# Squares of the residual and their sums, one to three positions later in the feed-forward pair of the second token half

## The chip, the cores and the metric

The kernel runs on one core of one Trainium2 chip. The metric is the device time of one execution in microseconds (us).

## The reference

One step of a decoder layer over 544 tokens: 512 of a new sequence and 8 x 4 tokens of running ones. What matters here is its second half (token mixing before it ends in `mix`, a matrix product):

```python
x = x + rmsnorm(mix, g_mix_post)
h = rmsnorm(x, g_ffn_pre)            # x * rsqrt(mean(x*x) + eps) * g
gt = h @ w_gate                      # 2048 -> 5632
c = conv_b + sum(ext(gt)[j] * conv_w[j] for j in range(3))
f = gelu(c) * (h @ w_up)
x = x + rmsnorm(f @ w_down, g_ffn_post)
```

## The kernel before

Activations lie with the 2048 model channels on the partitions, as 16 tiles (`kt`) of 128 x 544 tokens. Every fp32 product is made as three fast ones: weights and activations are split into a rounded part (`w_hi`, `act_hi`) and a rest (`w_lo`, `act_lo`), and `act_hi*w_hi`, `act_lo*w_hi` and `act_hi*w_lo` are summed in PSUM. Weights come in *units* of 128 x 512 numbers (two `kt` of a 256-column group), through a ring of four buffers: SP loads a unit, ACT makes `w_hi` (`split_hi`, line 358), DVE makes `w_lo` (`split_lo`, line 364), PE runs 24 matmuls of 272 columns on it. The buffers turn round: SP loads unit k+4 when DVE has split unit k, and ACT splits unit k+3 only when PE has used unit k-1 (`unit_used`).

Each engine has its own instruction queue, whose order is written out by hand: loops over positions k = 0 to 15, each of which begins with the split of unit k+3 (`LEAD` = 3) and then carries other work. Engines meet only at semaphores.

The change lies in the first feed-forward pair, 16 units that belong to two column groups (gate and up of 128 columns each). `PAIR` lays them out: units 0, 2, 4, 6, 8 and 10, 11, 12 are of the even group (banks `ps_acc`), 1, 3, 5, 7, 9 and 13, 14, 15 of the odd one (banks `ps_a`, `ps_b`). An even unit brings two new activation tiles (unit 8 needs kt 8 and 9, units 10, 11 and 12 need 10 to 15), an odd unit uses tiles that are there already. Units 0 to 3 run on the first token half, then on the second.

Beside this pair, the activations of the *second token half* (272 tokens) are prepared, in eight steps j = 0 to 7 of two tiles each:

- DVE `x2_pair(1, j)` (lines 1575, 1578): residual x2 = normalized mix + x.
- ACT `x2_hi(1, j)` (line 739): `act_hi` = rounded x2 * gain.
- DVE `x2_lo(1, j)` (line 1584): `act_lo`; this releases PE (`act_ready`).
- ACT `x2_squares(1, j)` (line 751): the squares of x2, into one of two buffers, `sq[:, j % 2]`.
- DVE `x2_add(1, j)` (line 1593 for j = 0, a copy; line 1596 for the others): adds them to `x2_sum`.

The buffers tie the last two: squares of j wait until the add of j-2 has read the buffer.

```python
def x2_squares(i, j):
    ...
        act.wait_ge(x2_added, 8 + max(j - 1, 0))
        dst = sq[:, j % 2]
```

The norm of the feed-forward input isn't applied to the activations but to the products: when all squares are summed, PE adds them over the partitions (`x2_sums`, line 939, after unit 12), DVE and ACT make the reciprocal root (`mean_square`, `root`, `root_mean`), PE spreads it (`spread_rstd`, line 910, after unit 13), DVE copies it to `rstd` (`rstd_in`, line 1235), and `gate_tail` (lines 1638 to 1661) takes the first gate and up products out of `ps_acc`, with the convolution, the GELU and the product. Then PE may use those banks again, from unit 16 on.

Of the kernel before, what the change touches and what calls it, by code (L numbers as in the profile page):

```python
# [74 lines left out]
PAIR_END = 12  # L75
# [72 lines left out]


FIRST_AT = {8 + 6 * j: j for j in range(8)}  # L150
ADD_AT = (1, 2, 4, 5, 7, 9, 11, 12)


ROWS_AT = {8 * s + 2 * mt + 1: s - 2 + mt for s in (2, 4, 6, 8) for mt in range(2)}
# [3 lines left out]
def build(nc, xT, units, kcache, vcache, table, gains, pool_hist, conv_par, rope_tab, consts,  # L158
          yT, kT_out, vT_out, ext_out, tail_out):
    with ExitStack() as ctx:  # L160
# [226 lines left out]
        def two(ap):  # L387
            return ap.rearrange("p (a n) -> p a n", a=2)
# [93 lines left out]
        def _(act):  # L482
# [259 lines left out]
            def x2_squares(i, j):  # L742

                if i == 0:
                    if j:
                        act.wait_ge(x2_added, j)
                    dst = sq_x
                else:
                    act.wait_ge(x2_added, 8 + max(j - 1, 0))
                    dst = sq[:, j % 2]  # L750
                act.activation(two(dst), x2[:, 2 * j:2 * j + 2, half_of(i)], ACT.Square).then_inc(x2_sq, 1)
# [32 lines left out]
            def chunk(c, first=False, last=False):  # L784
                q0 = c * Q_CH + Q_FF
                g0 = c * G_CH + G_FF

                def gate_group(j, before=None):
                    for u in range(8):
                        split_hi(act, 2 * j + q0, u + LEAD)  # L790
                        if before is not None and u == 1:
                            ff_gate(g0 + before, before)
                            f_part(before, before)
                    F = c * CH + j
                    ff_gate(j + g0, F)
                    f_part(F, j)
                if first:
                    split_hi(act, q0, LEAD)
                    half_out(HALVES - 1)
                    root(3, 4)  # L800
                    x2_hi(1, 0)
                    x2_hi(1, 1)
                    x2_squares(1, 0)
                    x2_squares(1, 1)
                    x2_hi(1, 2)
                    for k in range(1, 16):
                        split_hi(act, q0, k + LEAD)
                        if k == 1:
                            x2_squares(1, 2)
                        if k in (2, 4, 6, 8, 10):  # L810
                            x2_hi(1, k // 2 + 2)
                        if k in (3, 5, 7, 9, 11):
                            x2_squares(1, k // 2 + 2)
                        if k == PAIR_END:
                            root(4)
                        if k == PAIR_END + 2:
                            ff_gate(g0, 0)
                            f_part(0, 0)

                    gate_group(2, before=1)  # L820
                    gate_group(3)
                else:
                    with act.Fori(0, CH) as j:
                        gate_group(j)
                with act.Fori(0, 3 if last else 4) as d:
                    for k in range(4):
                        split_hi(act, d + q0 + 2 * CH, k + LEAD)
                    if last:
                        for i in range(4):
                            last_squares(4 * d + i, i % 2)  # L830
                if last:
                    split_hi(act, q0 + 2 * CH + 3, LEAD)
                    for i in range(4):
                        last_squares(12 + i, i % 2)
# [15 lines left out]
        def _(pe):  # L850
# [121 lines left out]
            def pair_halves(G, q):  # L972

                for k in (1, 0, 2, 3):
                    pair_half(q, k, 0)
                    if k == 0:
                        half_sums(1)
                half_spread(1)
                for k in range(4):
                    pair_half(q, k, 1).then_inc(unit_used, 1)  # L980
                for k in range(4, 16):
                    odd, u = PAIR[k]
                    ff_unit(G + odd, q, k, u, 8, act_hi, act_lo, odd, None if odd else lambda kt: (act_ready, 3 * KT + kt + 1))
                    if k == PAIR_END:
                        x2_sums()
                    if k == PAIR_END + 1:
                        spread_rstd(4)

            def pair_groups(G, q, n, ready):
# [217 lines left out]
        def _(dve):  # L1207
# [24 lines left out]
            def rstd_in(n):  # L1232

                dve.wait_ge(spread_done, n)
                dve.tensor_copy(rstd[:, :].rearrange("p (a n) -> p a n", a=4),
                                ps[:, :, :, HN:HN + NT // 4].rearrange("p a b n -> p (a b) n"))
                dve.drain().then_inc(rstd_ready, 1)
# [349 lines left out]
            def x2_add(i, j):  # L1587

                s = x2_sum[:, :, half_of(i)]
                dve.wait_ge(x2_sq, 8 * i + j + 1)  # L1590
                src = two(sq[:, j % 2] if i else sq_x)
                if j == 0:
                    dve.tensor_copy(s, src).then_inc(x2_added, 1)
                else:
                    dve.drain()
                    dve.tensor_tensor(s, s, src, ALU.add).then_inc(x2_added, 1)
# [67 lines left out]
            def chunk(c, first=False, last=False):  # L1664
                q0, g0 = c * Q_CH + Q_FF, c * G_CH + G_FF
                if first:
                    split_lo(dve, q0, LEAD)
                    add_half(HALVES - 1)
                    mean_square(3, ps[0:TOK, 0, 1, 0:4])
                    root_mean(3, 4)  # L1670
                    rstd_half(1)
                    x2_pair(1, 0)
                    x2_lo(1, 0)
                    x2_pair(1, 1)
                    x2_lo(1, 1)
                    x2_pair(1, 2)
                    for k in range(1, 16):
                        split_lo(dve, q0, k + LEAD)
                        if k in (1, 3, 5, 7, 9, 11):
                            x2_lo(1, k // 2 + 2)  # L1680
                        if k in (2, 4, 6, 8, 10):
                            x2_pair(1, k // 2 + 2)
                        if k in ADD_AT:
                            x2_add(1, ADD_AT.index(k))
                        if k == PAIR_END:
                            mean_square(4)
                        if k == PAIR_END + 1:
                            root_mean(4)
                            rstd_in(4)
                        if k == PAIR_END + 2:  # L1690
                            gate_tail(c, 0, 0, q0, PAIR_END)

                    gate_group(c, 2, 0, pair=True)
                    gate_group(c, 2, 1)
                else:
                    with dve.Fori(0, CH // 2) as j:
                        for odd in range(2):
                            gate_group(c, 2 * j, odd)

                def down(d, ahead):  # L1700
                    for k in range(4):
                        if k < ahead:
                            split_lo(dve, d + q0 + 2 * CH, k + LEAD)
                        if k >= 2:
                            for mt in range(2):
                                i, g = k - 2, 2 * d + g0 + CH + k - 2
                                t = tile_of(acc, 4 * d + 2 * i + mt)
                                tile_done(dve, g, mt, d + q0 + 2 * CH, k)
                                if first:
                                    o = dve.tensor_copy(two(t), bank(mt, i))  # L1710
                                else:
                                    o = dve.tensor_tensor(two(t), two(t), bank(mt, i), ALU.add)
                                o.then_inc(acc_free, 1)
                                if last:
                                    dve.drain().then_inc(mix_out, 1)
                    if last:
                        for i in range(4):
                            m = 4 * d + i
                            dve.drain()
                            dve.wait_ge(sq_done, m + KT + 1)  # L1720
                            dve.tensor_tensor(sq_sum, sq_sum, sq[:, i % 2], ALU.add).then_inc(sq_added, 1)
                if last:
                    dve.memset(sq_sum, 0.0)
                with dve.Fori(0, 3 if last else 4) as d:
                    down(d, 4)
                if last:
                    down(3, 1)
# [211 lines left out]
```

## Time and profile before

| | |
|---|---|
| median of 3 runs | 2470.76 us (2470.45 to 2473.14) |
| the profiled execution | 2472.72 us, its span 2470.9 us |
| TensorE clock granted over the span, mean | 0.989 of full speed |
| busy: PE, DVE, ACT | 2406.9, 1151.8, 732.2 us |

The profile is of one execution; its span leaves out what lies before the first and behind the last instruction. Busy times count an engine's instructions; PE at 97% says that PE sets the time, and that work of another engine counts only where PE waits for it. Such a place is found in a list of waits and then read in a timeline, where square brackets give the idle time ahead of an instruction and who ended it.

### The profile page before, as it was taken

The page shows a single profiled execution, that of the slowest core. Times are in us where ns is not written, and L with a number is a line of the kernel's source. Part 1 is how long each engine was busy: PE and PEld are TensorE (multiplying, and loading weights), DVE is VectorE, ACT ScalarE, POOL GpSimd, SP SyncE. Part 2 cuts the span into 40 slices and gives each one's busy share as a digit, 9 for nine tenths or more (in the row PEclk, how much of TensorE's full clock was granted, in tenths as well). Part 3 has the DMA queues.
Part 4 walks back from the last instruction along what each step waited for, and adds up shares of the span by engine and source line. Part 5 has one row for each costly group of instructions (what it writes and reads, how often), then busy time and mean ns, then how long its engine had stood idle before and what let it go on. Part 6 is the DMA issues. An engine that isn't in the chain of part 4 may idle for free.

```text
span 2470.9 us, 53021 instructions
## 1 busy us (share of the span) xinstructions
PE 2406.9 (97%) x20632; PEld 2331.7 (94%) x20632; DVE 1151.8 (47%) x1947; ACT 732.2 (30%) x1329; POOL 82.6 (3%) x244
## 2 busy tenths in 40 slices
PE   8999999999999999999999999999999999999994
PEld 8999988777999899999999999999999999999993
DVE  6633434346447654343444434344443434444357
ACT  5212322322456432222222222232322222232231
POOL 3000000000000000000000000000000000000002
PEclk9999999999999999999999999999999999999997
DMA  5499899997655322323232222323232232323321
GB/s 178 156 383 349 292 336 346 342 347 246 212 166 158 103 81 86 90 85 89 77 97 85 89 86 88 86 79 95 86 89 87 88 86 81 93 84 90 89 91 76
DMA packets 173165, 362.65 MB, mean 147 GB/s; under 512 B 19553, under 2 KB 19554, under 8 KB 172546
## 3 DMA queue, kind: packets, MB, share of 16 engines
q1 hardware_dynamic: 170978, 353.04, 44.0%
q0 software_dynamic: 2080, 8.14, 0.8%
q8 instruction: 73, 1.20, 0.2%
q14 instruction: 34, 0.28, 0.0%
HBM read 349.00 MB, written 12.10 MB: 146 GB/s over the span
## 4 chain that ended last, share of the span: by engine, by line
PE 92%; DVE 4%; DMA 1%; ACT 1%; issue 1%; DVEq 1%; SPq 0%; ACTq 0%
PE ps_acc L891 33%; PE ps_a L891 16%; PE ps_b L891 16%; PE ps_acc L868 13%; PE ps_acc L953 4%; PE ps_a L1089 2%; PE ps_a L1017 2%; DMA w_raw<-units 1%; DVE w_lo L364 1%; PE ps_b L1058 1%; PE ps_a L868 1%; PE ps_b L868 1%; ACT w_hi L358 1%; DVE region L1738 0%; PE ps_b L1048 0%
## 5 line engine op out<-in xcount | busy, mean ns | idle before, releaser
L364 DVE TENSOR_TENSOR w_lo<-w_raw,w_hi 128x512 fp32r<-128x512 f32 x780 | 533.6, 696 | 891.7 <-ACT w_hi L358 887.3
L358 ACT ACTIVATE w_hi<-w_raw 128x512 fp32r<-128x512 f32 x780 | 479.3, 627 | 1070.9 <-PE ps_acc L891 466.3
L891 PE MATMUL ps_acc<-act_hi,w_hi 128*128 128x272 f32 x1456 | 303.3, 290 | 12.7 <-DVE act_lo L1248 8.0
L891 PE MATMUL ps_acc<-act_lo,w_hi 128*128 128x272 f32 x1456 | 303.2, 289 | 0.0
L891 PE MATMUL ps_acc<-act_hi,w_lo 128*128 128x272 f32 x1456 | 301.1, 288 | 0.0
L891 PEld LDWEIGHTS ps_acc<-act_hi,w_hi 128*128 128x128 f32 x1456 | 229.5, 189 | 13.3 <-DVE w_lo L364 13.3
L891 PEld LDWEIGHTS ps_acc<-act_hi,w_lo 128*128 128x128 f32 x1456 | 230.6, 189 | 0.0
L891 PEld LDWEIGHTS ps_acc<-act_lo,w_hi 128*128 128x128 f32 x1456 | 230.2, 190 | 0.0
L868 PE MATMUL ps_acc<-act_hi,w_hi 128*128 128x272 f32 x832 | 180.6, 299 | 1.8 <-DVE scratch L1259 1.3
L868 PE MATMUL ps_acc<-act_hi,w_lo 128*128 128x272 f32 x832 | 172.2, 288 | 0.0
L868 PE MATMUL ps_acc<-act_lo,w_hi 128*128 128x272 f32 x832 | 172.2, 288 | 0.0
L891 PE MATMUL ps_a<-act_hi,w_hi 128*128 128x272 f32 x728 | 152.2, 290 | 0.0
L891 PE MATMUL ps_b<-act_lo,w_hi 128*128 128x272 f32 x728 | 151.3, 289 | 0.0
L891 PE MATMUL ps_a<-act_lo,w_hi 128*128 128x272 f32 x728 | 151.0, 289 | 0.0
L891 PE MATMUL ps_b<-act_hi,w_lo 128*128 128x272 f32 x728 | 150.6, 288 | 0.0
L891 PE MATMUL ps_b<-act_hi,w_hi 128*128 128x272 f32 x728 | 150.4, 288 | 0.0
L891 PE MATMUL ps_a<-act_hi,w_lo 128*128 128x272 f32 x728 | 150.1, 287 | 0.0
L891 PE MATMUL ps_acc<-f_hi,w_hi 128*128 128x272 f32 x704 | 145.6, 288 | 0.0
L891 PE MATMUL ps_acc<-f_lo,w_hi 128*128 128x272 f32 x704 | 145.3, 288 | 0.0
L891 PE MATMUL ps_acc<-f_hi,w_lo 128*128 128x272 f32 x704 | 145.0, 288 | 0.0
L868 PEld LDWEIGHTS ps_acc<-act_hi,w_hi 128*128 128x128 f32 x832 | 130.3, 190 | 13.3 <-issue 9.0
L953 PE MATMUL ps_acc<-act_hi,w_hi 128*128 128x272 f32 x448 | 130.9, 292 | 3.4 <-DVE w_lo L364 3.3
(270 smaller groups left out, 4207.0 us busy)
## 6 DMA issues: line engine op xcount, KB each, us to landing
w_raw<-units SPq DMA_DIRECT2D x780, 256.0 KB, 2.7
region<-kcache SPq DMA_DIRECT2D x128, 512.0 KB, 6.3
region<-vcache SPq DMA_DIRECT2D x256, 256.0 KB, 5.6
region<-xT SPq DMA_DIRECT2D x8, 544.0 KB, 6.9
region<-xT SPq DMA_DIRECT2D x4, 1088.0 KB, 8.5
yT<-region SPq DMA_DIRECT2D x8, 544.0 KB, 2.7
ext_out<-region POOLq DMA_DIRECT2D x8, 339.5 KB, 7.2
kT_out<-scratch POOLq DMA_DIRECT2D x8, 272.0 KB, 6.3
```

The source lines that it names most:

```text
L358: act.activation(w_hi[:, s], w_raw[:, s], ACT.Copy).then_inc(hi_ready, 1)
L364: dve.tensor_tensor(w_lo[:, s], w_raw[:, s], w_hi[:, s].bitcast(F32), ALU.subtract).then_inc(lo_ready, 1)
L868: mm = pe.matmul(banks(mt, odd)[:, n, 0:HN], w[:, s, i, cols], half(a[:, kt], n), start=kt == 0 and w is w_hi and a is hi, stop=kt == 2 * ...
L891: mm = pe.matmul(banks(mt, odd)[:, n, 0:HN], w[:, s, i, cols], half(a[:, kt], n), start=kt == 0 and w is w_hi and a is hi, stop=kt == 2 * ...
L953: mm = pe.matmul(ps[:, i % 2, mt, 0:HN], w[:, u % RING, j, mt * P:(mt + 1) * P], half(a[:, kt], i // 7), start=kt == 0 and w is w_hi and a ...
L1017: mm = pe.matmul(ps_a[quad * HC:(quad + 1) * HC, 0, r * P:(r + 1) * P], q_blk[:, h * HC:(h + 1) * HC], pages[:, slot, h * P:(h + 1) * P], ...
L1058: mm = pe.matmul(ps_b[:, 1, 0:P], v_toks[h // 2 % 2][:, h % 2, kj], probT[:, kj * P:(kj + 1) * P], start=kj == 0, stop=kj == qi)
L1089: mm = pe.matmul(ps_a[q * HC:(q + 1) * HC, 0 if f == 2 else 1, :], s_all[:, 4 * i + q, c:c + HC], halves[:, 4 * (turn % 4) + q, :], start= ...
```

## The change

Seven things are placed elsewhere in the three hand-written orders; no instruction is added or taken away.

```diff
-ADD_AT = (1, 2, 4, 5, 7, 9, 11, 12)
+ADD_AT = ((0, 3), (1, 5), (2, 7), (3, 9), (4, 11), (5, 12), (6, 13), (7, 13))
...
                     for k in range(1, 16):
                         split_hi(act, q0, k + LEAD)
-                        if k == 1:
-                            x2_squares(1, 2)
                         if k in (2, 4, 6, 8, 10):
                             x2_hi(1, k // 2 + 2)
                         if k in (3, 5, 7, 9, 11):
-                            x2_squares(1, k // 2 + 2)
-                        if k == PAIR_END:
+                            x2_squares(1, k // 2 + 1)
+                        if k == 12:
+                            x2_squares(1, 7)
+                        if k == PAIR_END + 2:
                             root(4)
-                        if k == PAIR_END + 2:
+                        if k == PAIR_END + 3:
                             ff_gate(g0, 0)
                             f_part(0, 0)
...
-                    if k == PAIR_END:
+                    if k == PAIR_END + 1:
                         x2_sums()
-                    if k == PAIR_END + 1:
+                    if k == PAIR_END + 2:
                         spread_rstd(4)
...
-                        if k in ADD_AT:
-                            x2_add(1, ADD_AT.index(k))
-                        if k == PAIR_END:
+                        for j, at in ADD_AT:
+                            if k == at:
+                                x2_add(1, j)
+                        if k == PAIR_END + 2:
                             mean_square(4)
-                        if k == PAIR_END + 1:
                             root_mean(4)
+                        if k == PAIR_END + 3:
                             rstd_in(4)
-                        if k == PAIR_END + 2:
                             gate_tail(c, 0, 0, q0, PAIR_END)
```

So squares 2 to 7 go from positions 1, 3, 5, 7, 9, 11 to 3, 5, 7, 9, 11, 12; adds 0 to 7 from 1, 2, 4, 5, 7, 9, 11, 12 to 3, 5, 7, 9, 11, 12, 13, 13; the sums over the partitions, the root, the spread and the first gate tail go one or two positions later.

ACT's queue before, from the last `x2_hi` ahead of position 1 on. L358 is a weight split, L739 an `x2_hi`, L751 a square:

```order
L739 ACTIVATE act_hi<-region2,gain 128x272 [waits x2_ready]
L739 ACTIVATE act_hi<-region2,gain 128x272
L358 ACTIVATE w_hi<-w_raw 128x512 [waits unit_used,w_loaded0]
L751 ACTIVATE scratch<-region2 128x544 [waits x2_added]
L358 ACTIVATE w_hi<-w_raw 128x512 [waits unit_used,w_loaded1]
L739 ACTIVATE act_hi<-region2,gain 128x272 [waits x2_ready]
```

ACT's queue in the changed kernel, at the same place:

```order
L358 ACTIVATE w_hi<-w_raw 128x512 [waits unit_used,w_loaded0]
L358 ACTIVATE w_hi<-w_raw 128x512 [waits unit_used,w_loaded1]
L739 ACTIVATE act_hi<-region2,gain 128x272 [waits x2_ready]
L739 ACTIVATE act_hi<-region2,gain 128x272
L358 ACTIVATE w_hi<-w_raw 128x512 [waits unit_used,w_loaded2]
L751 ACTIVATE scratch<-region2 128x544 [waits x2_added]
L358 ACTIVATE w_hi<-w_raw 128x512 [waits unit_used,w_loaded3]
```

The square with its wait on `x2_added` has left the place between the splits of units 4 and 5; the next one stands between those of units 6 and 7. From there on the sequence of kinds is the same as before, but the square at a position is of one step earlier, and so is the add that it waits for.

DVE's queue before, from position 2 to 4. L364 is a weight split, L1575 and L1578 are an `x2_pair`, L1584 an `x2_lo`, L1596 an add:

```order
L364 TENSOR_TENSOR w_lo<-w_raw,w_hi 128x512 [waits hi_ready]
L1575 TENSOR_TENSOR region1<-region1,rstd 128x2x272
L1578 TENSOR_TENSOR region2<-region1,region2 128x2x272
L1596 TENSOR_TENSOR shared<-shared,scratch 128x2x272 [waits x2_sq]
L364 TENSOR_TENSOR w_lo<-w_raw,w_hi 128x512 [waits hi_ready]
L1584 SCALAR_TENSOR_TENSOR act_lo<-region2,gain,act_hi 128x272 [waits act_hi_done] x2
L364 TENSOR_TENSOR w_lo<-w_raw,w_hi 128x512 [waits hi_ready]
```

DVE's queue in the changed kernel, from position 2 to 4:

```order
L364 TENSOR_TENSOR w_lo<-w_raw,w_hi 128x512 [waits hi_ready]
L1575 TENSOR_TENSOR region1<-region1,rstd 128x2x272
L1578 TENSOR_TENSOR region2<-region1,region2 128x2x272
L364 TENSOR_TENSOR w_lo<-w_raw,w_hi 128x512 [waits hi_ready]
L1584 SCALAR_TENSOR_TENSOR act_lo<-region2,gain,act_hi 128x272 [waits act_hi_done] x2
L1593 COPY shared<-scratch 128x2x272 [waits x2_sq]
L364 TENSOR_TENSOR w_lo<-w_raw,w_hi 128x512 [waits hi_ready]
```

Position 2 has lost its add, and position 3 has got the first one, the copy of step 0. Add 1 now stands at position 5, behind the `x2_lo` there, add 2 at 7 and add 3 at 9.

## Rows read from the trace of the kernel before

**Rows 1.** The page, part 1: busy time, share of the span, instructions of each engine.
```profile
PE 2406.9 (97%) x20632; PEld 2331.7 (94%) x20632; DVE 1151.8 (47%) x1947; ACT 732.2 (30%) x1329; POOL 82.6 (3%) x244
```

**Rows 2.** Who waited for whom, 818 to 900 us: total, times, longest (us).
```profile
PE ps_acc L891 <- DVE act_lo L1584: 4.7, 3, 2.6
```

**Rows 3.** Timeline of PE, 842 to 890 us: start, length, instruction [idle before].
```profile
842.15 0.43 PE L891 MATMUL ps_acc<-act_hi,w_hi 128*128 128x272 f32 x2
...
845.19 0.42 PE L891 MATMUL ps_a<-act_hi,w_hi 128*128 128x272 f32 x2
...
848.87 0.49 PE L891 MATMUL ps_acc<-act_hi,w_hi 128*128 128x272 f32 x2 [0.50 <-DVE act_lo L1584]
...
860.98 0.42 PE L891 MATMUL ps_acc<-act_hi,w_hi 128*128 128x272 f32 x2
...
865.74 0.49 PE L891 MATMUL ps_acc<-act_hi,w_hi 128*128 128x272 f32 x2 [1.58 <-DVE act_lo L1584]
...
871.63 0.55 PE L891 MATMUL ps_acc<-act_hi,w_hi 128*128 128x272 f32 x2 [2.63 <-DVE act_lo L1584]
...
876.25 2.08 PE L939 MATMUL ps_acc<-cst,shared 128*68 128x1 f32 x32
...
878.18 0.50 PE L891 MATMUL ps_a<-act_hi,w_hi 128*128 128x272 f32 x2
...
882.79 1.09 PE L910 MATMUL ps_acc<-scratch,cst 68*128 68x136 f32 x8
...
889.75 0.42 PE L891 MATMUL ps_acc<-act_hi,w_hi 128*128 128x272 f32 x2
```

**Rows 4.** Timeline of ACT, 842 to 844 us.
```profile
842.75 0.66 ACT L751 ACTIVATE scratch<-region 128x544 f32<-128x544 f32 x1 [1.94 <-DVE shared L1593]
843.32 0.61 ACT L358 ACTIVATE w_hi<-w_raw 128x512 fp32r<-128x512 f32 x1
```

**Rows 5.** Timeline of DVE, 841 to 871 us.
```profile
841.46 0.91 DVE L1584 SCALAR_TENSOR_TENSOR act_lo<-region,gain,act_hi 128x272 fp32r<-128x272 f32 x2
...
842.28 0.44 DVE L1593 COPY shared<-scratch 128x544 f32<-128x544 f32 x1
...
843.96 0.69 DVE L364 TENSOR_TENSOR w_lo<-w_raw,w_hi 128x512 fp32r<-128x512 f32 x1 [1.25 <-ACT w_hi L358]
...
844.57 0.72 DVE L1575 TENSOR_TENSOR region<-region,rstd 128x544 f32<-128x544 f32 x1
...
848.23 0.91 DVE L1584 SCALAR_TENSOR_TENSOR act_lo<-region,gain,act_hi 128x272 fp32r<-128x272 f32 x2
...
849.05 0.68 DVE L364 TENSOR_TENSOR w_lo<-w_raw,w_hi 128x512 fp32r<-128x512 f32 x1
...
853.30 0.91 DVE L1584 SCALAR_TENSOR_TENSOR act_lo<-region,gain,act_hi 128x272 fp32r<-128x272 f32 x2
...
854.31 0.72 DVE L1596 TENSOR_TENSOR shared<-shared,scratch 128x544 f32<-128x544 f32 x1
...
854.95 0.68 DVE L364 TENSOR_TENSOR w_lo<-w_raw,w_hi 128x512 fp32r<-128x512 f32 x1
...
859.20 0.91 DVE L1584 SCALAR_TENSOR_TENSOR act_lo<-region,gain,act_hi 128x272 fp32r<-128x272 f32 x2
...
870.99 0.91 DVE L1584 SCALAR_TENSOR_TENSOR act_lo<-region,gain,act_hi 128x272 fp32r<-128x272 f32 x2
```

**Rows 6.** Stretches: length, busy of PE, PEld, DVE, ACT, POOL, PEclk, DMA.
```profile
861.00:867.00 6.00, 4.42 (x36) 4.23 (x35) 4.31 (x8) 2.52 (x5) 0.00 (x0) 1.00 0.28 94
871.00:876.00 5.00, 4.37 (x23) 4.40 (x24) 2.95 (x6) 0.41 (x1) 0.00 (x0) 0.66 0.37 108
```

**Rows 7.** Timeline of DVE, 883 to 902 us.
```profile
883.92 0.72 DVE L1235 COPY rstd<-ps_acc 128x544 f32<-128x544 f32 x1 [2.28 <-PE ps_acc L910]
...
891.33 0.72 DVE L1661 TENSOR_TENSOR f_lo<-scratch,f_hi 128x544 fp32r<-128x544 f32 x1 [0.73 <-ACT f_hi L782]
...
900.70 1.28 DVE L364 TENSOR_TENSOR w_lo<-w_raw,w_hi 128x512 fp32r<-128x512 f32 x2
```

## The prediction

> **What bounds the kernel now.** I read the page's busy times first: PE is busy for 2406.9 us of the span, DVE for less than half of it [rows 1]. So PE sets the time, and a change that adds no instruction can only act where PE waits. The list of waits of the stretch comes next: PE waited three times, 4.7 us in all, for an `act_lo` of the second token half [rows 2]. The timeline of PE places them [rows 3]. A unit takes 845.19 - 842.15 = 3.04 us. Unit 6 starts at 848.87 behind a gap of 0.50, unit 11 at 865.74 behind 1.58, unit 12 at 871.63 behind 2.63. Units 10, 11 and 12 follow one another and each needs two new tiles, so there PE asks for a new step every 3.04 us, and DVE and ACT deliver one every (870.99 - 853.30) / 3 = 5.90 us [rows 5]. What counts is when `x2_lo(1, 7)` starts, at 870.99; unit 12 starts 0.64 later [rows 3, 5].
>
> Why 5.90, when DVE is not full? In each round of two positions DVE and ACT hand work to and fro: DVE makes x2, ACT rounds it, ACT splits the next weights, DVE makes the rests. ACT's squares and DVE's adds fill the gaps. The reader is to see in the DVE rows that an add is followed by the split of unit 9 after only 0.64 us (854.31 to 854.95) [rows 5]: ACT had made `w_hi` long before, because its square of that position waited for an *earlier* add.
>
> **The change, part by part.**
>
> *The square that leaves position 1* is a gain. There ACT stood still for 1.94 us until the first add (a copy) was done, then squared for 0.57 us before it split unit 5 (842.75 to 843.32), and DVE's split of unit 5 followed 0.64 later, at 843.96 [rows 4, 5]. Without it, ACT has unit 5 ready early, and DVE's split starts where the copy stood, 842.28. The pair of step 3 then starts 0.61 later (as 843.96 to 844.57), at 842.89 and not 844.57: 1.68 us earlier. `x2_lo(1, 3)` moves with it from 848.23 to 846.55 [rows 5], and unit 6 starts without a gap at 845.19 + 3.04 = 848.23, 0.64 us earlier than before [rows 3].
>
> *The first add at position 3* takes that back. It comes 0.82 behind `x2_lo` (as 841.46 to 842.28) [rows 5], at 847.37, and ends 0.44 later, at 847.81. ACT's next square waits for it and starts 0.03 later (842.72 to 842.75) [rows 4, 5], the split of unit 7 on ACT 0.57 behind that, and on DVE 0.64 behind that: 849.05. It was at 849.05 before [rows 5]. The whole 1.68 us is gone, and `x2_lo(1, 4)` stays at 853.30.
>
> *Adds 1, 2 and 3 at positions 5, 7 and 9* cost time. Squares 3, 4 and 5 stand at the same positions on ACT, and square j waits for add j-2: square 3 at position 5 for add 1 at position 5, and so on. Before, the add waited for stood one or two positions ahead. Behind the square, in ACT's queue, stands the weight split that DVE needs next. From the start of the add to the start of DVE's next split the path is now 0.72 (the add) + 0.03 + 0.57 (the square) + 0.64 (ACT's split, then DVE's) = 1.96 us, where it was 0.64 [rows 4, 5]: 1.32 us more a round. Three rounds lie between `x2_lo(1, 4)` and `x2_lo(1, 7)`: 3 x 1.32 = 3.96 us. The fourth such add, at position 11, stands behind `x2_lo(1, 7)` and can't delay unit 12. So `x2_lo(1, 5)` starts at 859.20 + 1.32 = 860.52, and unit 10 at 861.16 for 860.98; unit 11 at 865.74 + 2.64 = 868.38; unit 12 at 871.63 + 3.96 = **875.59** [rows 3, 5].
>
> *The clock.* Behind the wait of 1.58 us the granted clock stayed at 1.00 (2.4 GHz); behind 2.63 us it was 0.66 on average over 871 to 876, so 1.2 GHz for most of it [rows 6]. Unit 12 took 876.25 - 871.63 = 4.62 us, 1.58 over its 3.04; unit 13, behind the sums over the partitions, 882.79 - 878.18 = 4.61, 1.57 over [rows 3]. Now PE waits 868.38 - 861.16 - 3.04 = 4.2 us before unit 11, so I take unit 11 as slow, but 868.38 + 4.62 = 873.00 is still ahead of 875.59: hidden. Unit 12 again follows a wait of 2.6 us and is slow as before. The sums of 1.93 us (876.25 to 878.18) follow unit 13, and the slow unit is 14. I take the clock's cost as unchanged; one slow unit more or less, 1.6 us each way, goes to the range.
>
> *Sums, root and spread.* Adds 6 and 7 stand behind DVE's split of unit 16, which waits for PE to be done with unit 12. From there: 0.64 to DVE's split, 0.64 to an add, two adds of about 0.8 each, some 2.9 us, and a few tenths for the hand-overs, against 3.04 us of unit 13. I take a wait of 0.2 before the sums (0 to 0.5). The root has a unit of PE's work beside it, as before: 0.
>
> *The first gate tail* starts later against PE. Before, the copy of `rstd` began at 883.92, 5.83 us ahead of unit 16 at 889.75 [rows 3, 7]. Now unit 14 must end, ACT and DVE split unit 18 (1.3 to 1.7 us), and then comes the copy: about 2.2 us ahead of unit 16. PE needs the first bank some 1.7 us after the copy's start (0.84 to the next instruction, 0.85 for three small ones, by the same tail's pattern), so unit 16 is not held. Unit 21 needs its split behind both tails. From the copy to that split it took 900.70 - 883.92 = 16.8 us [rows 7], two weight splits fewer now (about 1.3): 15.5 at most, so it begins 13.3 us behind the start of unit 16 and is ready 0.7 later, at 14.0; PE comes there after 5 x 3.04 = 15.2. Cost 0, with 1.2 us to spare.
>
> **Sum.** 3.96 + 0.2 = +4.2 us on the profiled execution: 2476.9 for 2472.72. PE stays the bound behind the pair, so nothing gives it back. The median of the runs is 2.0 below the profiled execution; I put the same 4.2 on it: **2475.0 us**. A measurement of this kernel can tell about 0.2% (4.9 us) from no change, so the forecast lies just inside "same".
>
> A page speaks against any effect at all: the Trainium skill, "VectorE: DVE Perf Modes", Rules for kernel authors, says to minimise the count of Vector operations and not the semaphores. By it the sum would be 0, as the counts are equal. The trace differs in this place: of the 1.96 us only 0.72 is the add's own, the rest is what its semaphore holds on ACT.
>
> **Rivals.**
>
> *Nothing moves (2470.8).* DVE is at 47% and ACT at 30% [rows 1]; if the gaps in both took up the reordering, only the order of equal work would have changed. This is also what the page's rule gives. For it: the count. Against it: rows 5 show that DVE's gaps are waits for ACT's splits, which the change puts behind one more wait.
>
> *Faster (2467.5).* The wait taken from position 1 lasts, because the later squares find their buffers free in time. Unit 12 then starts 1.68 earlier; its wait falls to about 1 us, and behind 1.58 the clock stayed up, so unit 12 gains 1.58: 3.3 us. With the slow unit behind the sums gone too, 4.8. For it: the 1.94 us are really on the path. Against it: square 3 needs add 1, at its own position. It decides only if ACT reaches that square after the add.
>
> *Slower (2477.5).* The first gate tail holds PE at unit 16, whose banks it must empty. It bites once the copy of `rstd` begins less than 1.7 us ahead of unit 16; I reckon with 2.2, so 0.5 to spare. If the root or the split of unit 18 ahead of the copy comes a unit's time (3.04) later than I reckon, PE waits 2.5: 4.2 + 2.5 = +6.7 us, and 8.3 with a slow unit behind that wait. For it: 5.83 us ahead shrink to 2.2 [rows 3, 7]. Against: each part of the 2.2 has its row or pattern, and no queue has other work there.
>
> *The change does less than it says.* The buffers of the squares could make the order moot, but the queues' orders do differ where I read them; 2470.8 again.
>
> **Numbers.** Forecast 0.72, its own range +2.4 to +6.0 (one slow unit less or more), of which about two fifths lie over 4.9: 0.43 same, 0.29 slower. Nothing moves or no real change 0.14: same. Faster rival 0.07: 0.05 over 0.2% with the second slow unit, 0.02 same. Slower rival 0.07. Together faster 0.05, same 0.59, slower 0.36. The range takes in the forecast's own and most of both neighbours: 2471.2 to 2478.4.
>
> Of the clock, the Trainium skill, "TensorE: Matmul & The Clock Gate", Part 1, adds that how many matmuls run slow differs from run to run of the same kernel. No single trace can show that.
>
> **What would show it.** In the changed kernel's timelines: no ACT wait of 1.94 at the first square; unit 6 without a gap; the split behind each of adds 1, 2 and 3 some 1.96 us after the add's start; ACT's squares 3, 4 and 5 idle before them, released by `shared` L1596; step intervals of 7.2 us for 5.90; PE's gaps about 4.1 and 2.6 us before units 11 and 12; unit 12 starting 27.4 us after unit 6 for 22.8. If PE's waits for `act_lo` L1584 sum to no more than 4.7 us, the forecast is wrong; if PE waits for DVE at unit 16, the slower rival is right.

## The result

| | before | the changed kernel |
|---|---|---|
| median, 12 runs each | 2470.97 us (2469.63 to 2477.99) | 2477.35 us (2475.70 to 2482.64) |
| the profiled execution | 2472.72 us | 2476.84 us, its span 2475.1 us |
| TensorE clock over the span, mean | 0.989 | 0.988 |

The ratio is 1.0025, with a 95% interval of 1.0017 to 1.0034. That is 6.2 us slower, between 4.2 and 8.4: 0.25%, just over the bound of 0.2% that the prediction set. Between the two profiled executions it is 4.1 us: the one of the kernel before lies 1.75 us above the median of its runs, that of the changed kernel 0.5 below. In the experiments below, one kernel (one hold left) had two of its ten runs at a mean granted clock of 0.844 and 0.245, with 2618.7 and 9350.3 us, and its ratio leaves them out.

### The profile page after: what moved, and what is told of

It reads as the page before. It is cut to its first block, busy times and chain, and to the rows that moved or that the text cites. A ratio compares the mean times of both kernels' runs of the same rounds, so it can differ in the third digit from the quotient of the medians.

```text
span 2475.1 us, 53021 instructions
## 1 busy us (share of the span) xinstructions
PE 2408.9 (97%) x20632; PEld 2333.6 (94%) x20632; DVE 1152.0 (47%) x1947; ACT 732.5 (30%) x1329; POOL 82.4 (3%) x244
## 4 chain that ended last, share of the span: by engine, by line
PE 92%; DVE 4%; DMA 2%; ACT 1%; issue 1%; DVEq 1%; SPq 0%; ACTq 0%
PE ps_acc L891 32%; PE ps_a L891 16%; PE ps_b L891 16%; PE ps_acc L868 12%; PE ps_acc L953 5%; PE ps_a L1089 2%; PE ps_a L1017 2%; DVE w_lo L364 1%; PE ps_b L1058 1%; DMA region<-kcache 1%; DMA w_raw<-units 1%; PE ps_a L868 1%; PE ps_b L868 1%; ACT w_hi L358 1%; DVE region L1738 0%
## 5 line engine op out<-in xcount | busy, mean ns | idle before, releaser
L364 DVE TENSOR_TENSOR w_lo<-w_raw,w_hi 128x512 fp32r<-128x512 f32 x780 | 533.6, 696 | 899.9 <-ACT w_hi L358 895.5
L358 ACT ACTIVATE w_hi<-w_raw 128x512 fp32r<-128x512 f32 x780 | 479.1, 628 | 1070.8 <-PE ps_acc L891 464.2
```

Source lines behind the costliest of these rows:

```text
L358: act.activation(w_hi[:, s], w_raw[:, s], ACT.Copy).then_inc(hi_ready, 1)
L364: dve.tensor_tensor(w_lo[:, s], w_raw[:, s], w_hi[:, s].bitcast(F32), ALU.subtract).then_inc(lo_ready, 1)
```

## The profile after

The list of waits over the same stretch, 818 to 900 us (who waited for whom: total, times, longest, us), beside [rows 2]:

```profile
ACT scratch L751 <- DVE shared L1596: 11.2, 5, 2.4
...
PE ps_acc L891 <- DVE act_lo L1584: 7.1, 3, 4.0
...
ACT scratch L751 <- DVE shared L1593: 1.9, 1, 1.9
```

PE's waits for `act_lo` went from 4.7 to 7.1 us. The new line is the first: ACT's squares waited five times, 11.2 us in all, for an add. This line did not exist before; the one wait for the copy (L1593) is there in both kernels, at position 3 now.

PE's timeline (start, length, instruction [idle before]), beside [rows 3]. The rows are the starts of units 6, 10, 11, 12, 13, of the sums, of unit 14, of the spread and of unit 16:

```profile
847.65 0.42 PE L891 MATMUL ps_acc<-act_hi,w_hi 128*128 128x272 f32 x2
...
860.54 0.49 PE L891 MATMUL ps_acc<-act_hi,w_hi 128*128 128x272 f32 x2 [0.67 <-DVE act_lo L1584]
...
867.76 0.49 PE L891 MATMUL ps_acc<-act_hi,w_hi 128*128 128x272 f32 x2 [3.98 <-DVE act_lo L1584]
...
874.99 0.79 PE L891 MATMUL ps_acc<-act_hi,w_hi 128*128 128x272 f32 x2 [2.45 <-DVE act_lo L1584]
...
879.60 0.42 PE L891 MATMUL ps_a<-act_hi,w_hi 128*128 128x272 f32 x2
...
882.91 2.13 PE L939 MATMUL ps_acc<-cst,shared 128*68 128x1 f32 x32
...
884.90 0.53 PE L891 MATMUL ps_a<-act_hi,w_hi 128*128 128x272 f32 x2
...
889.52 1.09 PE L910 MATMUL ps_acc<-scratch,cst 68*128 68x136 f32 x8
...
893.47 0.47 PE L891 MATMUL ps_acc<-act_hi,w_hi 128*128 128x272 f32 x2
```

Unit 6 has lost its gap. Units 10, 11 and 12 wait 0.67, 3.98 and 2.45 us. Unit 12 takes 4.61 us (874.99 to 879.60), unit 14 takes 4.62. PE's waits for `act_lo` have grown by only 2.4 us; the rest of the delay stands in unit 11, which took 4.78 us (874.99 - 2.45 - 867.76) where it took 3.26 before (871.63 - 2.63 - 865.74) [rows 3].

One round on ACT: `x2_hi`, the split of unit 10, square 4, the split of unit 11.

```profile
857.80 0.94 ACT L739 ACTIVATE act_hi<-region,gain 128x272 fp32r<-128x272 f32 x2 [2.20 <-DVE region L1578]
858.64 0.62 ACT L358 ACTIVATE w_hi<-w_raw 128x512 fp32r<-128x512 f32 x1
861.66 0.66 ACT L751 ACTIVATE scratch<-region 128x544 f32<-128x544 f32 x1 [2.40 <-DVE shared L1596]
862.22 0.61 ACT L358 ACTIVATE w_hi<-w_raw 128x512 fp32r<-128x512 f32 x1
```

And the same round on DVE, beside [rows 5]; the last row is `x2_lo(1, 7)`:

```profile
859.29 0.69 DVE L364 TENSOR_TENSOR w_lo<-w_raw,w_hi 128x512 fp32r<-128x512 f32 x1 [1.52 <-ACT w_hi L358]
859.90 0.91 DVE L1584 SCALAR_TENSOR_TENSOR act_lo<-region,gain,act_hi 128x272 fp32r<-128x272 f32 x2
860.90 0.73 DVE L1596 TENSOR_TENSOR shared<-shared,scratch 128x544 f32<-128x544 f32 x1
862.87 0.69 DVE L364 TENSOR_TENSOR w_lo<-w_raw,w_hi 128x512 fp32r<-128x512 f32 x1 [1.25 <-ACT w_hi L358]
...
866.52 0.69 DVE L364 TENSOR_TENSOR w_lo<-w_raw,w_hi 128x512 fp32r<-128x512 f32 x1 [1.52 <-ACT w_hi L358]
867.13 0.91 DVE L1584 SCALAR_TENSOR_TENSOR act_lo<-region,gain,act_hi 128x272 fp32r<-128x272 f32 x2
...
874.35 0.91 DVE L1584 SCALAR_TENSOR_TENSOR act_lo<-region,gain,act_hi 128x272 fp32r<-128x272 f32 x2
```

Read from one to the other: add 2 runs from 860.90 to 861.63, square 4 starts on ACT at 861.66 behind 2.40 us of idleness, the split of unit 11 at 862.22, and DVE's split of it at 862.87. From the start of the add to DVE's next split it is 1.97 us, where it was 0.64 [rows 5]. A step takes 867.13 - 859.90 = 7.23 us for 5.90.

The granted clock in two stretches (length, busy of PE, PEld, DVE, ACT, POOL, PEclk, DMA), beside [rows 6]: in unit 11, behind the wait of 3.98 us, and in unit 14, behind the sums.

```profile
868.00:873.00 5.00, 4.53 (x24) 4.31 (x23) 2.81 (x5) 1.92 (x4) 0.00 (x0) 0.66 0.38 96
886.00:889.00 3.00, 3.00 (x16) 3.00 (x16) 1.05 (x3) 0.00 (x0) 0.00 (x0) 0.56 0.13 51
```

Both are partly at 1.2 GHz, as expected. Since unit 11 is slow while PE would have waited anyway, only units 12 and 14 cost time, as units 12 and 13 did before.

## The experiments

All compare with the kernel before, run on the same chip. One number is read from every trace: the time from the start of `x2_lo(1, 2)` to that of `x2_lo(1, 7)`. It leaves PE out, and so the clock of the matmuls. It was 870.99 - 841.46 = 29.53 us before [rows 5] and is 874.35 - 840.81 = 33.54 in the changed kernel.

The theories: **A**, ACT's square waits (the *hold*) for an add of its own position, and DVE's next split is queued behind it. **B**, the late adds or the late tail (sums, root, gate tail) make the loss by themselves. **C**, the clock does. **D**, added later: where unit 12 runs at full speed, PE waits for the last adds before the sums.

**Adds 0 to 4 one position earlier.**

```diff
-ADD_AT = ((0, 3), (1, 5), (2, 7), (3, 9), (4, 11), (5, 12), (6, 13), (7, 13))
+ADD_AT = ((0, 2), (1, 4), (2, 6), (3, 8), (4, 10), (5, 12), (6, 13), (7, 13))
```

> The changed kernel with adds 0 to 4 one position earlier each, at positions 2, 4, 6, 8, 10, behind the pair there; squares and tail stay late. Theory A (the loss is ACT's square waiting for an add of its own position): each add then falls into the gap in which DVE waits for ACT's split, the squares find their buffers free, steps come every 5.1 us for 7.2, unit 12 starts some 8 us earlier than in the changed kernel and 4 us earlier than in the kernel before, with a PE wait of about 1 us, so its clock stays up: 5 to 6 us faster than before (ratio about 0.9978). Theory B (the late tail of sums, root and first gate tail makes the loss): the tail is as late as in the changed kernel, so it stays about 4 us slower than before. Theory C (the longer waits only shift the clock's slow stretches): no clear difference from the changed kernel beyond 2 us.

Measured: ratio 0.9982 (0.9972 to 0.9991), 4.4 us *faster* than before, and 25.42 us between the two `x2_lo` (866.90 - 841.48). One round on DVE:

```profile
856.73 0.91 DVE L1584 SCALAR_TENSOR_TENSOR act_lo<-region,gain,act_hi 128x272 fp32r<-128x272 f32 x2
...
858.95 0.72 DVE L1578 TENSOR_TENSOR region<-region 128x544 f32<-128x544 f32 x1
859.77 0.73 DVE L1596 TENSOR_TENSOR shared<-shared,scratch 128x544 f32<-128x544 f32 x1
861.21 0.69 DVE L364 TENSOR_TENSOR w_lo<-w_raw,w_hi 128x512 fp32r<-128x512 f32 x1 [0.71 <-ACT w_hi L358]
861.82 0.91 DVE L1584 SCALAR_TENSOR_TENSOR act_lo<-region,gain,act_hi 128x272 fp32r<-128x272 f32 x2
```

The add (859.77) stands behind the pair, where DVE waits for ACT's split anyway: 0.71 us of that idleness are left. Steps come every 5.09 us. PE now waits once, 0.98 us, before unit 12 (rows: units 12, 13, the sums, unit 14):

```profile
867.54 0.49 PE L891 MATMUL ps_acc<-act_hi,w_hi 128*128 128x272 f32 x2 [0.98 <-DVE act_lo L1584]
...
870.64 0.42 PE L891 MATMUL ps_a<-act_hi,w_hi 128*128 128x272 f32 x2
...
873.95 2.13 PE L939 MATMUL ps_acc<-cst,shared 128*68 128x1 f32 x32
...
875.95 0.50 PE L891 MATMUL ps_a<-act_hi,w_hi 128*128 128x272 f32 x2
```

Unit 12 takes 3.10 us: the clock stayed up. Theory A stands; B and C would have kept this kernel slower than before.

**All adds at their old positions, squares and tail still late.**

```diff
+ADD_AT = ((0, 1), (1, 2), (2, 4), (3, 5), (4, 7), (5, 9), (6, 11), (7, 12))
```

> The changed kernel with all adds back at their old positions (1, 2, 4, 5, 7, 9, 11, 12); squares 2 to 7 stay late and so does the tail. Theory A: no square waits for an add of its position, steps come every 5.9 us as before, and the wait of 1.9 us at position 1 is gone: unit 12 about 1.1 us earlier than before, the whole 0.5 to 1 us faster than before (ratio 0.9997), thus 5 us or more faster than the changed kernel. Theory B: as slow as the changed kernel, +4 us or more over before.

Measured: 0.9991 (0.9982 to 1.0000), 28.20 us between the two `x2_lo`. The change's late squares and tail, without its late adds, do no harm.

**The tail alone**, in the kernel before:

```diff
-                        if k == PAIR_END:
+                        if k == PAIR_END + 2:
                             root(4)
-                        if k == PAIR_END + 2:
+                        if k == PAIR_END + 3:
                             ff_gate(g0, 0)
                             f_part(0, 0)
...
-                    if k == PAIR_END:
+                    if k == PAIR_END + 1:
                         x2_sums()
-                    if k == PAIR_END + 1:
+                    if k == PAIR_END + 2:
                         spread_rstd(4)
...
-                        if k == PAIR_END:
+                        if k == PAIR_END + 2:
                             mean_square(4)
-                        if k == PAIR_END + 1:
                             root_mean(4)
+                        if k == PAIR_END + 3:
                             rstd_in(4)
-                        if k == PAIR_END + 2:
                             gate_tail(c, 0, 0, q0, PAIR_END)
```

> The kernel before with only the sums, the root, the spread, the rstd copy and the first gate tail late, as in the change; squares and adds as before. Theory A: 0 to 0.5 us over before, unit 12 starts where it did; PE finds no wait at unit 16 over 0.3 us. Theory B: the whole loss, 4 to 6 us over before.

Measured: 0.9998 (0.9989 to 1.0007), 29.53 us as before. Unit 12 started 30.18 us behind `x2_lo(1, 2)` (30.17 before), and PE did not wait at unit 16. The tail's place costs nothing that can be measured.

**The first add ahead of position 1**, in the kernel before:

```diff
-ADD_AT = (1, 2, 4, 5, 7, 9, 11, 12)
+ADD_AT = (0, 2, 4, 5, 7, 9, 11, 12)
...
+                    x2_add(1, 0)
                     for k in range(1, 16):
```

> The kernel before with only the first add (the copy) moved ahead of position 1, into the gap in which DVE waits for ACT. It measures the gain that the prediction gave to the square that leaves position 1. Theory A: ACT no longer waits 1.9 us at square 2, step 3 and all behind it come 1.7 us earlier, unit 12 starts 1.7 us earlier: 1.7 us faster than before (ratio 0.9993), PE still waits over 1.6 us before unit 12 and its clock still falls. Rival: the 1.9 us are covered by later waits for PE's use of the ring, and nothing changes.

Measured: 0.9994 (0.9985 to 1.0003); 870.31 - 842.46 = 27.85 us, 1.68 less than before. That is to the hundredth the gain that the prediction gave to the square that leaves position 1. PE waited 2.54 us before unit 12, which took 4.61 us, and no longer waited before units 6 and 11. The time agrees with 1.7 us, but its interval holds no change too; the trace shows the gain, the runs alone don't.

**Four buffers for the squares.** Every instruction stays where the change put it:

```diff
-                    act.wait_ge(x2_added, 8 + max(j - 1, 0))
-                    dst = sq[:, j % 2]
+                    act.wait_ge(x2_added, 8 + max(j - 3, 0))
+                    dst = scratch[:, (0, 1, 3, 2)[j % 4], 0:NT]
```

> The changed kernel, every instruction at its place, but the squares turn through four buffers for two, so square j waits for add j-4. Theory A (the loss is the hold at the shared buffer, not the late place of squares and adds): ACT doesn't wait for an add any more; from the start of x2_lo(1, 2) to that of x2_lo(1, 7) it takes 5.1 + 5.5 + 3 x 5.9 = 28.3 us (29.5 before, 33.5 in the changed kernel); the whole about 1 us faster than before (ratio 0.9996). Theory B (late adds lengthen DVE's own work between two steps, whoever holds): 7.2 us a step and 33.5 us stay, 4 us or more slower than before.

Measured: 0.9997 (0.9988 to 1.0006), and 869.62 - 841.41 = 28.21 us. ACT's queue of the same round (`x2_hi`, split, square, split):

```profile
855.73 0.94 ACT L739 ACTIVATE act_hi<-region,gain 128x272 fp32r<-128x272 f32 x2 [3.37 <-DVE region L1578]
856.58 0.62 ACT L358 ACTIVATE w_hi<-w_raw 128x512 fp32r<-128x512 f32 x1
857.10 0.64 ACT L751 ACTIVATE scratch<-region 128x544 f32<-128x544 f32 x1
857.64 0.62 ACT L358 ACTIVATE w_hi<-w_raw 128x512 fp32r<-128x512 f32 x1
```

No idleness stands before the square, and DVE's split follows its add after 0.65 us again:

```profile
857.83 0.91 DVE L1584 SCALAR_TENSOR_TENSOR act_lo<-region,gain,act_hi 128x272 fp32r<-128x272 f32 x2
858.83 0.73 DVE L1596 TENSOR_TENSOR shared<-shared,scratch 128x544 f32<-128x544 f32 x1
859.48 0.69 DVE L364 TENSOR_TENSOR w_lo<-w_raw,w_hi 128x512 fp32r<-128x512 f32 x1
```

This is the sharpest of the tests: order and work are those of the changed kernel, only the buffer is free, and the loss is gone, where the changed kernel beside the same runs of the kernel before came to 1.0023 (1.0014 to 1.0032; below). B falls.

**One and two of the three holds taken away** (add 3 at 8 for 9; then add 2 at 6 for 7 as well):

```diff
+ADD_AT = ((0, 3), (1, 5), (2, 7), (3, 8), (4, 11), (5, 12), (6, 13), (7, 13))
```

> The changed kernel with add 3 alone one position earlier, at 8 for 9, so that one of the three holds is gone. Theory A: the last step takes 5.1 us for 7.2, the others stay; 31.4 us from x2_lo(1, 2) to x2_lo(1, 7) for 33.5; about 2 us over before. Theory B: unchanged at 33.5.

```diff
+ADD_AT = ((0, 3), (1, 5), (2, 6), (3, 8), (4, 11), (5, 12), (6, 13), (7, 13))
```

> The changed kernel with adds 2 and 3 one position earlier, at 6 and 8 for 7 and 9: two of the three holds gone. Theory A: 29.3 us from x2_lo(1, 2) to x2_lo(1, 7); within 1 us of before. Theory B: unchanged at 33.5.

| holds left | `x2_lo(1, 2)` to `x2_lo(1, 7)`, us | ratio to before (95%) |
|---|---|---|
| 3 (the changed kernel) | 33.54 | 1.0025 (1.0017 to 1.0034) |
| 2 | 31.38 | 1.0011 (1.0001 to 1.0020) |
| 1 | 29.25 | 1.0005 (0.9995 to 1.0015) |
| 0 (the first experiment, adds 0 and 4 earlier too) | 25.42 | 0.9982 (0.9972 to 0.9991) |

Each hold taken away gives back 2.15 us, as 7.23 us become 5.08. The four-buffer kernel, without the hold but with the add in its place, takes 5.90 us a step, so 1.33 of it is the hold and 0.82 the add that leaves the path. The last row has 1.68 more than one hold explains, the same as in the experiment on the first add.

In these two traces, with two holds and with one, PE also waited before the sums over the partitions (rows of the one, then of the other):

```profile
881.36 2.13 PE L939 MATMUL ps_acc<-cst,shared 128*68 128x1 f32 x32 [0.78 <-DVE shared L1596]
```

```profile
876.59 2.13 PE L939 MATMUL ps_acc<-cst,shared 128*68 128x1 f32 x32 [1.22 <-DVE shared L1596]
```

Both sums start 8.11 us behind `x2_lo(1, 7)` (873.25 and 868.48), and in both kernels unit 12 had run at full speed.

**The changed kernel once more.**

> The changed kernel once more, for its time against the kernel before on this chip and a second trace. The sum of the prediction says 4.2 us over before (ratio 1.0017); the first comparison said 1.0025. If the sum holds, the ratio comes to 1.0012 to 1.0022 and the trace shows PE waits of 0.7, 4.0 and 2.5 us before units 10, 11 and 12 again. If longer waits bring more slow stretches of the clock, as a rival for the rest, it stays at 1.0023 or more, the mean clock is lower than that of before by 0.001 or more, and the second trace has a slow stretch that the first has not.

Measured: 1.0023 (1.0014 to 1.0032); 874.66 - 841.12 = 33.54 us. So the first ratio was no chance: the two comparisons give 6.2 and 5.7 us. The forecast's 4.2 is the lower end of the first interval and lies inside the second (3.5 to 7.9), so a loss beyond it is likely and not shown. What was written above for the sum (a ratio up to 1.0022, waits of 0.7, 4.0 and 2.5 us) did not come; the signs named for the clock did: the ratio, a mean clock of 0.9883 for 0.9896 before, and a stretch, unit 14, that was slower than in the first trace. The 33.54 us are the same in both traces. The second trace shows where more can go (rows: units 11 and 12, the sums, unit 14, the spread):

```profile
868.07 0.79 PE L891 MATMUL ps_acc<-act_hi,w_hi 128*128 128x272 f32 x2 [3.93 <-DVE act_lo L1584]
...
875.30 0.49 PE L891 MATMUL ps_acc<-act_hi,w_hi 128*128 128x272 f32 x2 [1.45 <-DVE act_lo L1584]
...
882.76 2.60 PE L939 MATMUL ps_acc<-cst,shared 128*68 128x1 f32 x32 [1.21 <-DVE shared L1596]
...
885.23 0.80 PE L891 MATMUL ps_a<-act_hi,w_hi 128*128 128x272 f32 x2
...
890.81 1.21 PE L910 MATMUL ps_acc<-scratch,cst 68*128 68x136 f32 x8
```

Unit 11 was slow throughout here (5.78 us), and so PE waited only 1.45 us before unit 12, and the clock stayed up in unit 12 (3.08 us, as unit 13 began at 878.38). But then PE waited 1.21 us before the sums, for the last add, and behind them all of 885 to 889 was at 1.2 GHz:

```profile
885.00:889.00 4.00, 4.00 (x21) 4.00 (x20) 1.58 (x6) 0.21 (x1) 0.00 (x0) 0.50 0.13 46
```

Unit 14 took 5.58 us for 3.04. In the first trace the slow unit 12 had hidden most of that wait: the sums started 3.31 us after unit 13, 0.27 more than a unit at full speed.

**The last adds earlier**, with the three holds left in: theory D.

```diff
+ADD_AT = ((0, 3), (1, 5), (2, 7), (3, 9), (4, 11), (5, 11), (6, 12), (7, 13))
```

> The changed kernel with its two sorts of loss taken apart: the three holds stay (adds 1, 2, 3 at 5, 7, 9), and only the last adds come earlier: add 5 at 11 for 12, add 6 at 12 for 13. Theory D (in executions where the clock doesn't fall in unit 12, PE waits about 1.2 us before the sums over the partitions for the last add, which lies a fixed 8.1 us behind the start of x2_lo(1, 7), and that is the part which the prediction put at 0.2): no wait of PE before the sums, x2_lo(1, 2) to x2_lo(1, 7) still 33.5 us, 1 to 2 us faster than the changed kernel, so about 4 us over before (ratio 1.0012 to 1.0020). Rival (the rest beyond the sum is the clock or chance alone): no wait goes, the ratio stays at 1.0023 to 1.0026.

Measured: 1.0017 (1.0008 to 1.0026), 33.53 us. DVE from `x2_lo(1, 7)` on: adds 4, 5, 6 and 7.

```profile
875.64 0.91 DVE L1584 SCALAR_TENSOR_TENSOR act_lo<-region,gain,act_hi 128x272 fp32r<-128x272 f32 x2
876.64 0.72 DVE L1596 TENSOR_TENSOR shared<-shared,scratch 128x544 f32<-128x544 f32 x1
877.81 0.72 DVE L1596 TENSOR_TENSOR shared<-shared,scratch 128x544 f32<-128x544 f32 x1 [0.44 <-issue]
...
879.39 0.72 DVE L1596 TENSOR_TENSOR shared<-shared,scratch 128x544 f32<-128x544 f32 x1
...
882.60 0.72 DVE L1596 TENSOR_TENSOR shared<-shared,scratch 128x544 f32<-128x544 f32 x1
```

The sums start at 883.90 without a wait, 3.01 us after unit 13 (3.31 in the changed kernel's first trace, 4.38 in its second). The ratio moved the right way and to the expected place, but the intervals overlap, and in this execution unit 12 was slow, so the wait of 1.2 us would not have shown in full. Unit 14 ran at full speed in this trace, 3.08 us for 4.62 in the changed kernel's first; whether the edit or chance kept it there is not shown. That the wait before the sums exists is shown: 8.10 or 8.11 us from `x2_lo(1, 7)` to the sums in three traces, and 7.05 without a wait in the four-buffer kernel, whose last squares wait for no add (876.67 - 869.62, unit 12 at full speed there too). What it is worth in the time of the runs is not settled.

**Both together.**

```diff
+ADD_AT = ((0, 2), (1, 4), (2, 6), (3, 8), (4, 10), (5, 11), (6, 12), (7, 13))
```

> The kernel with adds 0 to 4 at the even positions, where no square waits and DVE's gap takes them, and the last three at 11, 12 and 13. Theory A and D together: 25.4 us from x2_lo(1, 2) to x2_lo(1, 7), one PE wait of 1.0 us before unit 12 and none before the sums, 4 to 6 us faster than before (ratio 0.9976 to 0.9984), as the first experiment, whose sums were not held either. Rival: no gain over before beyond 2 us in this second comparison.

Measured: **0.9971** (0.9961 to 0.9982), 2465.46 us: 7.2 us faster than before, in a span of 2465.1. From `x2_lo(1, 2)` to `x2_lo(1, 7)` it takes 25.42 us, PE waits 1.09 us before unit 12, and the clock stayed up from unit 4 on. This version beats both kernels. That it is better than the first experiment is not shown: their intervals overlap.

## Why the prediction was right, and where it was off

*The square that leaves position 1* (1.68 us earlier): right. `x2_lo(1, 3)` came 5.08 us after `x2_lo(1, 2)` for 6.77, and the experiment on the first add gave 1.68 by itself in its trace.

*The first add at position 3* (takes it all back): right. `x2_lo(1, 4)` came 11.85 us after `x2_lo(1, 2)`, 11.84 before.

*Three holds of 1.32* (3.96 us): right. Steps of 7.24, 7.23 and 7.22 us for 5.90, 5.90 and 5.89 are 4.0 us in all. The four-buffer kernel shows that it is the hold and not the place; the series of holds shows that it adds up.

*Nothing moves, by the count of Vector operations*: the rival fell. The counts are equal in both kernels, and DVE's and ACT's busy times are within 0.3 us of before (PE's is 2.0 us longer, 2408.9 us). The Trainium skill, "VectorE: DVE Perf Modes", Rules for kernel authors, puts the count over the semaphores for chained Vector operations. Here, where the semaphore ties two engines together, the count did not decide. One semaphore held ACT for 2.40 us four times and 1.57 us once, and three of these holds put 1.32 us each on the path to unit 12.

*The clock, taken as unchanged*: right for the two profiled executions (two slow units on the path in each), not shown for the runs. The changed kernel's 23 runs have a mean clock of 0.9880, the 82 runs of the kernel before beside the experiments 0.9896; but that takes in unit 11's slow stretch, which falls into a wait and costs nothing, so it does not say what the clock cost.

*The wait before the sums, 0.2 (0 to 0.5)*: this is the term that was mis-sized for executions in which unit 12 runs at full speed: 1.2 us in the second trace. I hung the last adds on PE's use of unit 12. That is so only where unit 12 is slow (0.3 us measured in the first trace). Where it is not, the chain that holds is the other one that I had written off: add 4 at position 11, square 6, the split of unit 15, add 5, square 7, the split of unit 16, adds 6 and 7. It ends 8.1 us behind the start of `x2_lo(1, 7)`, and PE, with two units at full speed, is there 1.2 us earlier. So the changed kernel waits for its last adds for most of what a full-speed unit 12 would have saved (1.2 of 1.5 us). The prediction said that the hold at position 11 "can't delay unit 12"; true, but it delays the sums.

*The first gate tail*: right by luck. Unit 16 started at 893.47 without a wait, but the spare 0.5 us was nearly used up: DVE's third small instruction on the first bank ended at 893.30, 0.17 us ahead. Behind the copy of `rstd` I had counted 0.84 us to the next instruction; it was 1.40, because DVE waited 0.69 us for POOL, which writes the convolution's history into the same tile once `rstd` is there:

```profile
891.05 0.72 DVE L1235 COPY rstd<-ps_acc 128x544 f32<-128x544 f32 x1
892.45 0.44 DVE L1638 TENSOR_TENSOR scratch<-ps_acc,rstd 128x272 f32<-128x272 f32 x1 [0.69 <-POOL scratch L1808]
```

Before, the split of unit 17 stood between them and covered it. I had named ACT and PE there and left out POOL.

*The faster and slower rivals*: the faster one needed square 3 to come after its add; ACT was always there first. Its sum was off as well: with step 3 earlier by 1.68 us, the wait before unit 12 did not fall to about 1 us but stayed at 2.54, and the waits before units 6 and 11 went instead. The slower one had the wrong place, as PE did not wait at unit 16; the only additional wait came at the sums. Its 2477.5 us lies next to the measured 2477.35 by coincidence.

The forecast's size was 4.2 us with a bound of 4.9 for "same". Measured were 6.2 by the ratio and 6.4 between the medians: beyond the forecast's own range, which ended at 6.0, and inside the stated one only because that was widened for the rivals. By the prediction's own bound the likeliest label, "same" (0.59), was not what came, though the interval, 0.17% to 0.34%, holds both. So the mechanism is right, and the size is right in the traces and small for the runs. With the sums' wait at 1.2 for executions without a slow unit 12, the sum for these is 5.2, and the label would have been open; what makes the last 1 us of the difference is not shown.

## What to carry to other kernels

When two queues share a double buffer, the release must stand *ahead* of the position at which the other engine needs the buffer, or there must be more buffers, as the kernel with four shows. At the same position the two engines run in turn, and what is queued behind the waiting instruction pays, here the weight split that PE's supply of activations needs. A filler instruction belongs into the gap in which its engine waits for the other one anyway: here behind the pair, not behind `x2_lo`. And when a chain has two possible holders (PE's use of a unit, or the chain of adds and squares), both sums have to be made for each state of the clock, since a slow stretch that hides one of them is not there in every execution.

## What the runs showed of the hardware that was not expected

The same wait of PE before unit 12 ended in different clocks. In the kernel before it was 2.63 us, and the granted clock was 0.66 over the next 5 us [rows 3, 6]. With the adds at their old positions it was 2.63 us too, and the clock stayed at 1.00:

```profile
871.50 0.49 PE L891 MATMUL ps_acc<-act_hi,w_hi 128*128 128x272 f32 x2 [2.63 <-DVE act_lo L1584]
```

```profile
871.00:876.00 5.00, 4.50 (x36) 4.54 (x37) 3.31 (x6) 1.46 (x3) 0.00 (x0) 1.00 0.39 108
```

In the changed kernel, 3.98 us before unit 11 were followed by a clock of 0.66 over 868 to 873, and 1.45 us before unit 12, in the second trace, by full speed. Two more traces fall on either side: behind 2.65 us unit 12 took 4.61 us with the tail alone moved, and 3.10 us with four buffers. So in these traces the length of the wait doesn't settle whether the next unit runs at 1.2 or 2.4 GHz. The Trainium skill, "TensorE: Matmul & The Clock Gate", Part 1, says that the number of slow matmuls differs from run to run of the same kernel; the two traces of the changed kernel agree, with 4.61 and 3.08 us for unit 12. What that is worth in the time of a whole run stays open: the runs of the kernel before lie between 2468.6 and 2478.0 us, and only profiled executions tell where their clock fell.
